# Two key groups as the two heads of a pair: scores on the row halves of the array, compressed branch once per query tile

## What is computed

```python
s_c = jnp.einsum('bqghd,bngd->bghqn', qg, k_cmp)          # 63 compressed keys
p_c = masked_softmax(s_c, cmp_end[None, :] <= tq[:, None])
imp = jnp.einsum('bghqn,nj->bgqj', p_c, overlap)           # summed over the heads of a group
...
_, idx = lax.top_k(score, n_sel)                           # 8 blocks of 64 keys, per query and group
...
p_s = masked_softmax(s_s, mask_s)                          # selected blocks
...
p_w = masked_softmax(s_w, mask_w)                          # the last 512 keys
o = gc[..., 0:1] * o_c + gc[..., 1:2] * o_s + gc[..., 2:3] * o_w
```

## Time and profile before

| | |
|---|---|
| median of 3 executions | 2973.07 us (2971.09 to 2973.86) |
| profiled execution, its own time | 2975.5 us |
| span of the profile | 2973.7 us |
| PE busy | 2909.8 us, 98% |
| DVE, ACT, POOL busy | 67%, 48%, 16% |
| mean granted clock of PE | 0.990 of full speed |

### The profile page before, as it was taken

One profiled execution on the slowest core, in us unless ns is written; L12 is line 12 of the kernel. 1 busy time (PEld: TensorE's weight loads), 2 busy tenths in 40 slices (PEclk: granted clock), 3 DMA queues, 4 the chain that ended last, 5 costly groups with the idle time before them and its releaser, 6 DMA issues.

```text
span 2973.7 us, 42637 instructions
## 1 busy us (share of the span) xinstructions
PE 2909.8 (98%) x16332; PEld 2413.5 (81%) x16332; DVE 1984.1 (67%) x3262; ACT 1441.8 (48%) x2411; POOL 467.7 (16%) x764
## 2 busy tenths in 40 slices
PE   9999999889999999999999999999999999999998
PEld 6888888778988887888878888777877788888887
DVE  6653246766775349999989852475654877778864
ACT  4552125887776126555444431375643544444432
POOL 0110004765554120000000010261012000000000
PEclk9999997999999999999999999999999999999999
DMA  4222231000000511333344332000101244464232
GB/s 150 73 84 71 85 114 43 2 1 2 2 2 7 207 43 64 114 114 114 114 160 157 116 111 92 28 2 36 43 30 72 104 165 168 157 241 156 99 114 71
DMA packets 85383, 262.14 MB, mean 88 GB/s; under 512 B 10448, under 2 KB 13648, under 8 KB 84800
## 3 DMA queue, kind: packets, MB, share of 16 engines
q1 hardware_dynamic: 74208, 219.29, 20.3%
q0 software_dynamic: 10976, 40.15, 3.8%
HBM read 187.58 MB, written 66.06 MB: 85 GB/s over the span
## 4 chain that ended last, share of the span: by engine, by line
PE 89%; DVE 4%; ACT 4%; issue 2%; POOL 0%; DMA 0%; SPq 0%; ACTq 0%; DVEq 0%; POOLq 0%
PE PS L256 33%; PE PS L3136 23%; PE PS L3158 12%; PE PS L919 3%; PE PS L933 3%; PE PS L905 2%; PE PS L904 2%; PE PS L280 1%; PE PS L1563 1%; PE PS L1598 1%; PE PS L1585 1%; ACT P_SHORT L1003 1%; PE PS L956 1%; PE PS L3187 1%; ACT PT L1013 1%
## 5 line engine op out<-in xcount | busy, mean ns | idle before, releaser
L223 ACT CAST WHI<-RAW 128x1024 fp32r<-128x1024 f32 x100 | 104.8, 1049 | 589.4 <-PE PS L256 569.6
L228 DVE TENSOR_TENSOR WLO<-RAW,WHI 128x1024 fp32r<-128x1024 f32 x102 | 125.5, 1231 | 361.4 <-ACT WHI L223 360.1
L256 PE MATMUL PS<-HLO,WHI 128*128 128x512 f32 x992 | 306.2, 390 | 0.0
L3136 PE MATMUL PS<-XSH_T,PWH 128*128 128x512 f32 x596 | 233.1, 391 | 5.4 <-DVE PWL L2396 2.4
L3136 PE MATMUL PS<-XSH_T,PWL 128*128 128x512 f32 x596 | 231.9, 389 | 0.0
L3136 PE MATMUL PS<-XSL_T,PWH 128*128 128x512 f32 x596 | 231.9, 389 | 0.0
L3158 PE MATMUL PS<-DXH,PWH 128*128 128x512 f32 x560 | 218.1, 389 | 1.4 <-DVE DXL L2620 1.3
L256 PEld LDWEIGHTS PS<-HLO,WHI 128*128 128x128 f32 x992 | 186.5, 188 | 39.2
L3158 PE MATMUL PS<-DXL,PWH 128*128 128x512 f32 x560 | 217.9, 389 | 0.0
L3158 PE MATMUL PS<-DXH,PWL 128*128 128x512 f32 x560 | 217.9, 389 | 0.0
L3136 PE MATMUL PS<-XSH_B,PWL 128*128 128x512 f32 x456 | 177.4, 389 | 0.0
(11 more groups left out here) (443 smaller groups left out, 7225.6 us busy)
## 6 DMA issues: line engine op xcount, KB each, us to landing
W<-in_w SPq DMA_DIRECT2D x57, 1024.0 KB, 6.4
RAW<-in_w SPq DMA_DIRECT2D x104, 512.0 KB, 3.3
hidden<-W SPq DMA_DIRECT2D x54, 512.0 KB, 2.8
DXR<-hidden_t SPq DMA_DIRECT2D x20, 1024.0 KB, 5.1
DXR<-hidden SPq DMA_DIRECT2D x15, 1024.0 KB, 5.1
hidden_t<-W SPq DMA_DIRECT2D x24, 512.0 KB, 3.3
hidden_t<-T SPq DMA_DIRECT2D x16, 512.0 KB, 3.1
PLAIN_RAW<-hidden SPq DMA_DIRECT2D x14, 512.0 KB, 4.2
```

The lines of the kernel that those rows point to most:

```text
L223: nc.scalar.copy(WHI[:, slot, :], RAW[:, slot, :]).then_inc(w_hi, 1)
L228: nc.vector.tensor_tensor(WLO[:, slot, :], RAW[:, slot, :], WHI[:, slot, :].bitcast(F32), ALU.subtract).then_inc(w_lo, 1)
L256: last = nc.tensor.matmul(o[:, half], w[:, slot, cols], x(k)[:, half], start=(k == 0 and w is WHI and x is hi), stop=(done and k == kcs - ...
L3136: last = nc.tensor.matmul(c.banks[q % 2][b], wt[n % 4][:, cols], xt[x][:, k, :], start=(opens and k == 0 and xt is c.xsh and wt is c.pwh), ...
```

## The change

A pair is now head j of group 0 with head j of group 1, and a query tile is one segment of 8 pairs; its pairs are m = 8 qt + j. QHI, QLO, KHI and KLO hold both groups, each on its own 64 partitions, for all three products high x high, high x low, low x high. Each is a pair of matmuls over 64 rows, one per group, that write different PSUM banks. Scores now come by branch (both groups of the selected branch, then both of the window), and a span over 512 columns is cut near its middle (parts_of). The compressed branch runs once per tile for both groups, on tiles twice as wide, with its steps at pairs 0 to 5 of the tile before; the gate multiplies EC in place after the choice. Outputs are split with one instruction per pair on 128 partitions, and the key and query splits take half as many instructions. ACT's and POOL's loops follow (ACT: out, cmp and query steps at the same places of the tile; act_cmp_exp at pair 2).

```diff
...
+    KHI = sb("KHI", [2, T], R + 56 * KB, F32R)
+    KLO = sb("KLO", [2, T], R + 40 * KB, F32R)
+    QHI = [sb(f"QHI{i}", [HPG, P], X_AT + 8 * KB * i, F32R) for i in range(2)]
+    QLO = [sb(f"QLO{i}", [HPG, P], X_AT + 8 * KB * i + 4 * KB, F32R) for i in range(2)]
+    N_KEYS = 2
...
+    def dve_keys_lo(dve, branch):
+        dve.wait_ge(k_hi, branch + 1)
+        nc.vector.tensor_tensor(KLO[:, branch, :], KF[:, branch, :], KHI[:, branch, :].bitcast(F32),
+                                ALU.subtract).then_inc(k_lo, 1)
...
+        w = width_of(m, branch)
+        first = w if short(m) else w // 2 // P * P
+        return [(0, first), (first, w)] if first < w else [(0, w)]
+
+    def scores_of(m, branch, g):
+
+        if short(m):
+            return PS[:, T * branch + 512 * g:T * branch + 512 * g + 512]
+        start = T * g + 512 - parts_of(m, branch)[0][1]
+        return PS[:, start:start + width_of(m, branch)]
...
+    def pe_scores(pe, m, branch):
+
+        qt, j = qt_of(m), m % HPG
+        pe.wait_ge(q_lo, qt + 1)
+        if not short(m):
+            pe.wait_ge(shifted, 4 * m + 2 * branch)
+        elif m:
+            pe.wait_ge(shifted, 4 * (m - 1) + 2 * branch + 2)
+        lo = P * max(0, qt - 4) if branch else 0
+        q_hi_t, q_lo_t = QHI[qt % 2], QLO[qt % 2]
+        for c, end in parts_of(m, branch):
+            keys = slice(lo + c, lo + end)
+            for q, k in ((q_hi_t, KHI), (q_hi_t, KLO), (q_lo_t, KHI)):
+                for g in range(N_GROUPS):
+                    rows = half_of(g)
+                    last = nc.tensor.matmul(scores_of(m, branch, g)[:, c:end], q[rows, j, :], k[rows, branch, keys],
+                                            start=(q is q_hi_t and k is KHI), stop=(q is q_lo_t))
+        last.then_inc(s_done, 1)
...
         for h in range(HPG):
-            last = nc.tensor.matmul(out[:, HEAD * h:HEAD * h + HEAD], Q[:, h, P * qt:P * qt + P], KCZ[g][:, :],
-                                    start=True, stop=True)
-        last.then_inc(t_done if s else c_mm, 1)
...
+            for g in range(N_GROUPS):
+                last = nc.tensor.matmul(outs[g][:, HEAD * h:HEAD * h + HEAD], Q[half_of(g), h, P * qt:P * qt + P],
+                                        KCZ[g][half_of(g), :], start=True, stop=True)
+                if qt and h == HPG - 1:
+                    last.then_inc(t_done, 1)
...
             if ahead:
-                pe_scores(pe, 2 * ahead)
+                pe_scores(pe, ahead, 0)
...
+            if next_tile(m, 5):
+                pe_cmp_turn(pe, next_tile(m, 5))
+            if next_tile(m, 0):
+                pe_cmp_scores(pe, next_tile(m, 0))
...
             if ahead and not waits_for_all(m):
-                pe_scores(pe, 2 * ahead + 1)
+                pe_scores(pe, ahead, 1)
...
     def act_out_hi(act, m):
         act.wait_ge(pv_done, used_at[m + 1])
-        for e in range(2):
-            nc.scalar.copy(out_of(O_HI, m, e), out_ps(m)[half_of(e), :]).then_inc(o_hi, 1)
+        nc.scalar.copy(out_of(O_HI, m), out_ps(m)).then_inc(o_hi, 1)
 
     def act_attention(act):
...
+    def pool_cmp_gate(pool, qt):
+        pool.wait_ge(c_bias, qt + 1)
+        nc.gpsimd.tensor_tensor(EC_ALL, EC_ALL, cmp_gates(qt), ALU.mult).then_inc(c_gated, 1)
...
-            if m in MASKED:
-                pool_mask(pool, MASKED[m])
-            if m in SUMMED:
-                pool_cmp_gate(pool, SUMMED[m])
-            if m in SCORED:
-                pool_cmp_shift(pool, SCORED[m])
+            if next_tile(m, 1):
+                pool_cmp_mask(pool, next_tile(m, 1))
+            if next_tile(m, 2):
+                pool_cmp_shift(pool, next_tile(m, 2))
+            if next_tile(m, 4):
+                pool_cmp_gate(pool, next_tile(m, 4))
+                pool_mask(pool, next_tile(m, 4), 0)
+            if next_tile(m, 5):
+                pool_mask(pool, next_tile(m, 5), 1)
             if ahead:
-                pool_probs(pool, 2 * ahead)
-                pool_probs(pool, 2 * ahead + 1)
...
+                pool_probs(pool, ahead, 0)
+            if next_tile(m, 3):
+                pool_cmp_probs(pool, next_tile(m, 3))
+            if ahead:
+                pool_probs(pool, ahead, 1)
...
+    def dve_select(dve, qt):
+
+        if qt:
+            dve.wait_ge(c_probs, qt)
+        seq(dve, nc.vector.tensor_reduce(IMPC[:, :, :], EC[:, :, :, :].rearrange("p g h n -> p g n h"), AX.X, ALU.add))
...
     def dve_cmp_first(dve):
...
-        seq(dve, nc.vector.tensor_tensor(EC[:, :, :], EC[:, :, :], per_head(CINV[:, :]), ALU.mult))
-        gates = GATE[:, qt, 0:3 * HPG].rearrange("p (h b) -> p h b", b=3)[:, :, 0]
-        nc.vector.tensor_tensor(PCG[:, :, :], EC[:, :, :], per_head(gates), ALU.mult).then_inc(c_gated, 1)
+        seq(dve, nc.vector.tensor_tensor(EC_ALL, EC_ALL, per_head(CINV[:, :]), ALU.mult))
         dve_select(dve, 0)
+        nc.vector.tensor_tensor(EC_ALL, EC_ALL, cmp_gates(0), ALU.mult).then_inc(c_gated, 1)
         dve.wait_ge(c_bias, 1)
-        seq(dve, nc.vector.tensor_copy(MSEL[0][:, 0:P].rearrange("p (j l) -> p j l", l=SLC),
-                                       SBIAS[:, 0:2].unsqueeze(2).to_broadcast([P, 2, SLC])))
-        seq(dve, nc.vector.tensor_tensor(MSEL[0][:, 0:P], MSEL[0][:, 0:P], TRI[:, :], ALU.add))
+        for g in range(N_GROUPS):
+            last = nc.vector.tensor_copy(MSEL[g][:, 0:P].rearrange("p (j l) -> p j l", l=SLC),
+                                         SBIAS[:, g, 0:2].unsqueeze(2).to_broadcast([P, 2, SLC]))
+        seq(dve, last)
+        for g in range(N_GROUPS):
+            last = nc.vector.tensor_tensor(MSEL[g][:, 0:P], MSEL[g][:, 0:P], TRI[:, :], ALU.add)
+        seq(dve, last)
...
     def dve_out_lo(dve, m):
-        for e in range(2):
-            dve.wait_ge(o_hi, 2 * m + e + 1)
-            last = nc.vector.tensor_tensor(out_of(HLO, m, e), out_ps(m)[half_of(e), :],
-                                           out_of(O_HI, m, e).bitcast(F32), ALU.subtract)
-        last.then_inc(o_free, 1)
+        dve.wait_ge(o_hi, m + 1)
+        nc.vector.tensor_tensor(out_of(HLO, m), out_ps(m), out_of(O_HI, m).bitcast(F32), ALU.subtract)\
+            .then_inc(o_free, 1)
...
             if ahead:
-                dve_shift(dve, 2 * ahead, 0)
-                dve_shift(dve, 2 * ahead, 1)
-            if m >= PAIRS_SHORT:
+                dve_shift(dve, ahead, 0, 0)
+                dve_shift(dve, ahead, 0, 1)
+            if not short(m):
                 dve_out_lo(dve, m - 1)
-            if m in SUMMED:
-                dve_cmp_sum(dve, SUMMED[m])
-            if m in SCORED:
-                dve_cmp_min(dve, SCORED[m])
-            if m in SELECTED:
-                dve_select(dve, SELECTED[m])
-            if m >= PAIRS_SHORT and next_seg(m, 1):
-                dve_queries_lo(dve, next_seg(m, 1))
+            if next_tile(m, 3):
+                dve_cmp_sum(dve, next_tile(m, 3))
+            if not short(m) and next_tile(m, 4):
+                dve_queries_lo(dve, next_tile(m, 4))
             if ahead:
-                dve_shift(dve, 2 * ahead + 1, 0)
-                dve_inverse(dve, 2 * ahead)
-                dve_shift(dve, 2 * ahead + 1, 1)
-            if 0 < m < PAIRS_SHORT:
+                dve_shift(dve, ahead, 1, 0)
+                dve_inverse(dve, ahead, 0)
+                dve_shift(dve, ahead, 1, 1)
...
-            if m < PAIRS_SHORT and next_seg(m, 0):
-                dve_queries_lo(dve, next_seg(m, 0))
+            if short(m) and next_tile(m, 3):
+                dve_queries_lo(dve, next_tile(m, 3))
+            if next_tile(m, 1):
+                dve_cmp_min(dve, next_tile(m, 1))
+            if next_tile(m, 3):
+                dve_select(dve, next_tile(m, 3))
...
```

More of the change, by code:

```diff
@@ L692, in dve_compress @@
         if t in (4, 5):
-            for g in range(N_GROUPS):
-                dve_keys_lo(dve, g, t == 5)
+            dve_keys_lo(dve, t - 4)
         if t == 4:
@@ L714, in act_compress @@
         if t in (3, 4):
-            for g in range(N_GROUPS):
-                act_keys_hi(act, g, t == 4)
+            act_keys_hi(act, t - 3)
         if t == 5:
@@ L889, in waits_for_all @@
         return m + 1 == PAIRS_SHORT
-    def pe_scores(pe, n):
-        s, qt, g, j = where(n)
-        pe.wait_ge(q_lo, s + 1)
-        for branch in range(2):
-            if not short(n):
-                pe.wait_ge(shifted, 2 * n - 1 + branch)
-            elif n >= 2:
-                pe.wait_ge(shifted, 2 * n - 3 + branch)
-            lo, hi = (P * max(0, qt - 4) if branch else 0), P * qt + P
-            for c in range(lo, hi, 512):
-                end = min(c + 512, hi)
-                out = scores_of(n, branch)[:, c - lo:end - lo]
-                nc.tensor.matmul(out, QS[s % 2][:, j, :], KHD[g][:, branch, c:end], start=True, stop=False)
-                last = nc.tensor.matmul(out, QS[s % 2][:, j, :], KLD[g][:, branch, c:end], start=False, stop=True)
-            last.then_inc(s_done, 1)
```

(37 more changed lines are left out.)

388 lines of the change are left out of this document (175 added, 213 removed).

## The result

The changed kernel took 2986.98 us (median of 5 executions, 2984.04 to 2989.69) against 2973.86 for the kernel before on the same chip (5 executions): a ratio of 1.0043, 95% interval 1.0028 to 1.0057. It is slower by 0.4%. The forecast was 2971 us, a change of 2 us that can't be told from none; 2987 lies inside its range (2953 to 2988), but on the wrong side. The profiled execution took 2985.14 us, and its span is 9.7 us longer than the one before, not 13; what follows is read from those two traces.

The account below looks back on a forecast made before the run. PE's list was taken to bound tiles 4 to 6, and in-order lists with a busy ACT tiles 0 to 2. Terms -14.0 - 4.8 + 15 + 1.5 + 1 + 2.5 + 6.0 - 9.1 = -1.9 us gave 2971 us, range 2953 to 2988.

Parts of the forecast that it names:

- the short tiles: Tiles 0 to 3: ACT's shorter list outweighs one choice partly hidden by running two pairs ahead; -9.1 us, bounds -18 and 0.
- The start: Ahead of tile 0: DVE's wider first compressed softmax delays KF's evacuation while PE stands; +6.0 us.
- The long tiles: Tiles 4 to 7: savings on scores against waits for the late choice, the minimum, chunk copies and PE's clock.
- The choice: Tiles 4 to 6: PE waits about 5 us each behind DVE's doubled choice, +15 us; lower PE clock after it, +2.5.
- -14.0: Tiles 4 to 7: selected and window scores on two row halves side by side, less two more shape changes per pair.
- -4.8: Tiles 4 to 6: one block of compressed scores per tile falls away, less a change of shape; 1.6 us each.
- +1.5: Tiles 4 to 6: the minimum at the end of pair 1's round makes PE wait about 0.5 us.
- +1: Tile 7: four chunks go into three banks, and their copies queue behind the later exponential; 1 us.
- Scores and shapes: PE's scores: fp32r row halves run side by side at half the serial time; each change of array shape costs 0.18 us.
- Rivals 3 and 4: fp32r halves not side by side, about 3050 us, chance 0.05; or only in part, 2990 us, chance 0.01.
- Rival 1: The choice is hidden in DVE's idle time, without the waits and their clock: 2954 us, chance 0.20.
- Rival 2: PE's clock: 10 us at half clock after each of three waits, and a slower tile 0; 2986 us, chance 0.20.

Follow-up runs that it names:

- x1: Changed kernel with the choice of blocks left out from tile 1 on, masks staying those of the first selection: 0.9948 of the kernel before.
- x7: Changed kernel with DVE evacuating KF's last tile ahead of the first choice, gate and masks: 1.0048 of the kernel before.
- x16: Changed kernel with extra PE matmuls in the waits for the choice, 12 per short tile and 24 per long tile: 1.0009 of the kernel before.
- x13: Changed kernel with 29 extra PE matmuls while PE waits for KF's evacuation at the start: 1.0035 of the kernel before.
- x12: Changed kernel with low queries split at pair 5, not 4, and the last short output split ahead of pair 32's shifts: 1.0046 of the kernel before.
- x10: Changed kernel with zeros written in place of the choice in tiles 0 to 3: 0.9992 of the kernel before.
- x14: Kernel before with the choice skipped in tiles 0 to 3, as x10 does in the changed kernel: 0.9997 of the kernel before.

## Why the prediction was wrong

**The step that failed** is the one called "the short tiles": "against that stands one choice with its wait for POOL, some 7 us of DVE in one round ... Running two pairs ahead hides part", -9.1 us in sum. Measured: +3.7. The prediction had priced the same wait at 4.9 us in tile 4; it charged tile 1 with 1.5 us of it and let tile 2 hide it. The runs show 15.3 us for the choice in tiles 0 to 3, as much per tile as in the long tiles. Running ahead hides nothing here, and the order gives a reason: ACT's exponential for the pair two ahead stands in front of ACT's other work and waits for the shift behind the choice. The waits of 4.2 to 5.4 us on ACT fit it; no run moves that exponential, so the reason is read and not tested. This one term is 12.8 of the 13.8 us between forecast (-1.9) and trace (+5.9 for the start, +3.7, and +2.3 for the long tiles).

A second part of the same step was wrong and doesn't show in the sum. The 3.3 us per tile that ACT's shorter list should give did not come where ACT was taken to set the pace:

| us against before | tile 0 | tile 1 | tile 2 | tile 3 | sum |
|---|---|---|---|---|---|
| forecast | -3.5 | -1.8 | -3.3 | -0.5 | -9.1 |
| changed kernel | -1.3 | +3.5 | +3.3 | -1.8 | +3.7 |
| without the choice (x1) | -4.7 | -0.4 | -0.9 | -5.6 | -11.6 |

Without the choice the sum is near the forecast without its 1.5 us (-10.6), but by luck: tiles 1 and 2 gave far less and tile 3 more. In tile 1 ACT's busy time fell from 35.8 to 32.2 us and the tile only from 39.3 to 38.9, so ACT's work alone did not set its length.

**The start** came out right in sum: +6.0 forecast; from PE's first compressed scores to the first output the profiles show 30.7 us before and 36.6 after. The piece that was worked out, DVE's chain up to the evacuation of KF, grew by 4.7 us and not 6.0, and so did the time to the first scores; the other 1.2 us came between the first scores and the first output, where the forecast had nothing. That the first score matmul came at 475.65 and not near 478.7 is this 1.3 and an offset of 1.8 ahead of it: PE's first compressed scores start between 455.5 and 457.7 us in these profiles. x7 shows that KF is not the only path: PE's scores 5.1 us earlier gave 1.0.

**The long tiles** came out at +2.3 us, forecast +1.2, but by two errors that cancel. The choice: 15 for the waits and 2.5 for the clock were forecast, 12.3 measured for both. The chain in tile 6 ran as it was worked out. From T = 847.30, the end of the selected scores, POOL was done at T + 9.3 (forecast 9.7), the choice at T + 13.0 (13.8), the shifts at T + 15.1 (16.0), and PE wanted them at T + 11.5 (11.0): 3.7 us in place of 5.0; the waits in tiles 4 and 5 were 3.2 and 3.8. All else: -16.3 forecast (-14.0, -4.8, +1.5, +1), -10.0 measured (x1 against before). Tile 4 stands out, 3.5 us longer without the choice where 4.5 shorter was forecast (5.0 saved, 0.5 lost to the minimum), but part of that is where the tiles are cut: its window still has two blocks of compressed scores, as before, while tile 3's has none where it had two. Both tiles together gave 2.1 us without the choice where 5.0 were forecast. At pair 32 PE waited before as well, 2.98 us for the split of an output, with 3.4 us of half clock behind it; now it waits 1.83 us for a minimum and 1.87 for that split, and the half clock behind it lasts 6.8 us. The first of these rows is from the kernel before, the others are the changed kernel's:

```profile
667.12 2.19 PE L919 MATMUL PS<-IDENT,P_LONG 128*128 128x128 f32 x12 [2.98 <-DVE HLO L1217]
...
673.62 0.39 PE L905 MATMUL PS<-KHI,QHI 64*128 64x256 f32 x2 [1.83 <-DVE HMIN L1101]
...
676.63 3.68 PE L958 MATMUL PS<-KCZ,Q 64*128 64x64 f32 x32 [1.87 <-DVE HLO L1238]
680.24 2.71 PE L920 MATMUL PS<-IDENT,P_LONG 128*128 128x128 f32 x12
```

At full clock these 32 take 2.00 us, one block for both groups against 1.89 for one before. Tile 7 gave 4.5 us, more than the 2.9 forecast.

**Scores and shapes** stand as forecast: both row halves run side by side, a window block of (256, 384) takes 1.15 us, and scores start 0.07 before the transposes end (852.91 + 1.53 against 854.37). Rivals 3 and 4 did not happen. Rival 1, the hidden choice at 2954, did not either; without any choice (x1) the kernel takes 2959. Rival 2 was right in kind: the clock behind the waits costs some 10 us in all seven tiles (x16), where the sum had 2.5 for three. That its 2986 is next to the measured 2987 is luck: it asked for some 7 us of half clock or more behind each wait of the long tiles and found 3.4, 6.8 and 3.4, and what it had not in it, the choice in the short tiles, made up the rest. With 10 in place of 2.5 the forecast's sum would have been +5.6, still within 0.2%. These 10 us are no further term of the account above: they lie inside the tiles' 15.3 and 12.3.

What stays open: whether filling the start is worth anything in the changed kernel itself (x13), how the miss of tiles 3 and 4 divides between the waits at pair 32 and their clock, since x12 moved the wait and lost the gain again, and what sets the length of tiles 1 and 2 when there is no choice.

## What to carry to other kernels

When work is merged to save fixed costs, its longest piece doubles and its wait moves; price that piece at every place where it stands, not only where the profile shows a full engine, by following what queues behind it in each in-order list. Look first at the order on the helper engine: letting POOL do the awaited operation ahead of its routine ones gave 17 us for a move of two lines. And ask whether the long piece is needed at all: half of the choices left nothing out, and skipping them gave 15 us here (x10), though nothing in the kernel before, where they were hidden (x14).
